# Scaling probabilities on GpSimd, copying turned probabilities on VectorE

## The reference

```python
pc = softmax(where(valid_c, q_raw @ kc.T * SCALE, NEG))        # compressed keys
ps = softmax(where(mask_s, q_rot @ k_slc.T * SCALE, NEG))      # selected blocks
pw = softmax(where(mask_w, q_rot @ k_win.T * SCALE, NEG))      # window of 512
o  = g[0] * (pc @ vc) + g[1] * (ps @ v_slc) + g[2] * (pw @ v_win)
```

## Time and profile before

| | |
|---|---|
| median of three executions | 3274.55 us |
| the profiled execution | 3271.69 us |
| its span in the trace | 3269.9 us |
| mean granted TensorE clock | 0.994 |
| PE busy | 3204.8 us (98%) |
| DVE busy | 1168.0 us (36%) |
| ACT busy | 1176.9 us (36%) |
| POOL busy | 1456.7 us (45%) |

### The profile page before, as it was taken

How to read it: one execution, slowest core, us unless ns; L and a number is a source line. 1 busy time by engine, 2 the same in 40 slices (tenths; PEclk the granted TensorE clock), 3 DMA queues, 4 the chain that set the end, 5 groups by cost and what they waited for, 6 DMA issues and landing times.

```text
span 3269.9 us, 39586 instructions
## 1 busy us (share of the span) xinstructions
PE 3204.8 (98%) x15940; PEld 2636.8 (81%) x15940; DVE 1168.0 (36%) x1727; ACT 1176.9 (36%) x1388; POOL 1456.7 (45%) x1112
## 2 busy tenths in 40 slices
PE   8999999999999999999999999999999989999998
PEld 7878888888888888888776888888888877788887
DVE  6534331343434112211847522114221375652212
ACT  4544332433443233222427332224222243743322
POOL 4335545433545444444550354454444373054443
PEclk9999999999999999999999999999999999999999
DMA  4213222211222222223320122222222242022222
GB/s 149 76 52 116 90 103 103 103 57 66 102 90 103 103 102 92 102 91 112 133 79 25 57 111 91 102 103 90 100 93 103 83 148 79 13 91 90 103 99 94
DMA packets 46234, 302.56 MB, mean 93 GB/s; under 512 B 5392, under 2 KB 7440, under 8 KB 10784
## 3 DMA queue, kind: packets, MB, share of 16 engines
q1 hardware_dynamic: 41040, 292.79, 25.0%
q10 hardware_dynamic: 5072, 7.96, 0.9%
HBM read 296.54 MB, written 2.10 MB: 91 GB/s over the span
## 4 chain that ended last, share of the span: by engine, by line
PE 90%; DVE 6%; ACT 2%; DMA 1%; issue 0%; SPq 0%; DVEq 0%; ACTq 0%
PE main L424 73%; PE main L441 3%; PE main L567 2%; PE main L1907 1%; PE main L526 1%; PE main L527 1%; PE main L531 1%; PE misc L527 1%; PE misc L526 1%; PE misc L531 1%; PE misc L484 1%; ACT b_p L2061 1%; PE misc L499 1%; DMA stage<-in_w 1%; DVE b_p L2283 1%; DVE b_flat L2146 1%
## 5 line engine op out<-in xcount | busy, mean ns | idle before, releaser
L2379 POOL TENSOR_TENSOR w_lo<-stage,w_hi 128x512 fp32r<-128x512 f32 x1104 | 1450.7, 1347 | 1778.8 <-ACT w_hi L637 1778.8
L424 PE MATMUL main<-h_hi,w_lo 128*128 128x512 f32 x2456 | 965.2, 393 | 7.3 <-DVE val L2093 5.5
L424 PE MATMUL main<-h_hi,w_hi 128*128 128x512 f32 x2456 | 959.3, 391 | 0.0
L424 PE MATMUL main<-h_lo,w_hi 128*128 128x512 f32 x2456 | 959.2, 391 | 0.0
L637 ACT ACTIVATE w_hi<-stage 128x2048 fp32r<-128x2048 f32 x276 | 525.0, 1910 | 408.3 <-DMA stage<-in_w 407.5
L424 PEld LDWEIGHTS main<-h_hi,w_lo 128*128 128x128 f32 x2456 | 463.6, 189 | 109.8 <-DVE val L2093 6.0
L424 PEld LDWEIGHTS main<-h_hi,w_hi 128*128 128x128 f32 x2456 | 463.0, 189 | 97.5
L424 PEld LDWEIGHTS main<-h_lo,w_hi 128*128 128x128 f32 x2456 | 463.6, 189 | 95.3 <-issue 0.5
L424 PE MATMUL main<-hid_hi,w_lo 128*128 128x512 f32 x1168 | 454.5, 389 | 0.0
L424 PE MATMUL main<-hid_hi,w_hi 128*128 128x512 f32 x1168 | 454.4, 389 | 0.0
L424 PE MATMUL main<-hid_lo,w_hi 128*128 128x512 f32 x1168 | 454.4, 389 | 0.0
(11 more groups left out here) (337 smaller groups left out, 3190.2 us busy)
## 6 DMA issues: line engine op xcount, KB each, us to landing
stage<-in_w SPq DMA_DIRECT2D x276, 1024.0 KB, 4.8
x<-in_xT SPq DMA_DIRECT2D x4, 512.0 KB, 7.6
out_x<-x ACTq DMA_DIRECT2D x4, 512.0 KB, 2.7
stage<-in_w SPq DMA_DIRECT2D x4, 256.0 KB, 7.8
b_r<-sq ACTq DMA_DIRECT2D x4, 256.0 KB, 6.8
b_r<-sq ACTq DMA_DIRECT2D x4, 255.5 KB, 8.2
ev_ws<-in_ev_ws ACTq DMA_DIRECT2D x1, 512.0 KB, 4.8
b_pos<-in_pos ACTq DMA_DIRECT2D x2, 256.0 KB, 2.8
```

The lines of the kernel that those rows point to most:

```text
L424: last = pe.matmul(acc[:, m, :], w[a], r[b], start=start and k == 0 and j == 0, stop=stop and k == nk - 1 and j == 2)
L2379: last = e.tensor_tensor(c.w_lo[:, s, k:k + 2, :].rearrange("p k n -> p (k n)"), c.stage[:, s, k * CW:(k + 2) * CW], c.w_hi[:, s, k:k + 2, ...
```

## The change

GpSimd does the scaling of line 2258. VectorE signals `a_share` behind the product with the gate, and GpSimd signals `a_norm` for each head as VectorE did. ScalarE copies only head 0 of each turned step (`a_copied`). VectorE copies head 1 in the new `turned`, behind `shares(s-1)` (`a_copied_b`). TensorE's waits follow the new counts. GpSimd's loop over chunks is cut in three: up to the attention of each layer it makes the low parts of all chunks whose high parts ScalarE has made by then, scales, and goes on.

```diff
@@ nsa_tensor, turn and values
-            pe.wait_ge(c.a_copied, 50 * l + 2 * s + hh + 1)
+            if hh == 0 or s == 0:
+                pe.wait_ge(c.a_copied, 26 * l + s + 1 + (s > 0 or hh))
+            else:
+                pe.wait_ge(c.a_copied_b, N_STEPS * l + s)
...
-        pe.wait_ge(c.a_copied, 50 * l + 2 * s + 4)
+        pe.wait_ge(c.a_copied, 26 * l + s + 3)
+        pe.wait_ge(c.a_copied_b, N_STEPS * l + s + 1)
@@ nsa_scalar
-            for hh in range(2):
-                act.wait_ge(c.a_probT, 50 * l + 2 * s - 2 + hh + 1)
-                act.activation(c.b_pT[:, (s - 2) % 2, hh, 0:w], c.m[hh][:, 0:w], ACT.Copy).then_inc(c.a_copied, 1)
+            act.wait_ge(c.a_probT, 50 * l + 2 * s - 1)
+            act.activation(c.b_pT[:, (s - 2) % 2, 0, 0:w], c.m[0][:, 0:w], ACT.Copy).then_inc(c.a_copied, 1)
@@ nsa_vector, shares
-        step(dve.tensor_tensor(den, den, gate, ALU.mult))
-        for hh in range(2):
-            for r, br in enumerate(brs):
-                p = step_prob(c, s, hh, r)
-                u = 2 * hh + br
-                last = dve.tensor_scalar(p, p, c.b_den[:, s % 4, u:u + 1], None, ALU.mult)
-            last.then_inc(c.a_norm, 1)
+        dve.tensor_tensor(den, den, gate, ALU.mult).then_inc(c.a_share, 1)
+
+    def turned(s):
+        i, m, brs = STEPS[s]
+        w = (i + 1) * P * len(brs)
+        dve.wait_ge(c.a_probT, 50 * l + 2 * s + 4)
+        dve.tensor_copy(c.b_pT[:, s % 2, 1, 0:w], c.m[1][:, 0:w]).then_inc(c.a_copied_b, 1)
...
+        if 2 <= s < N_STEPS + 2:
+            turned(s - 2)
@@ GpSimd
+def nsa_pool(pool, c, l):
+    for s in range(N_STEPS):
+        i, m, brs = STEPS[s]
+        pool.wait_ge(c.a_share, N_STEPS * l + s + 1)
+        for hh in range(2):
+            for r, br in enumerate(brs):
+                u = 2 * hh + br
+                p = step_prob(c, s, hh, r)
+                last = pool.tensor_scalar(p, p, c.b_den[:, s % 4, u:u + 1], None, ALU.mult)
+            last.then_inc(c.a_norm, 1)
...
+            made = seen = 0
+            for kind, kw in plan:
+                seen += PHASE_CHUNKS[kind]
+                if kind == "nsa":
+                    low_parts(made, seen - 4 + AHEAD)
+                    made = seen - 4 + AHEAD
+                    nsa_pool(pool, c, kw["l"])
+            low_parts(made, n_chunks)
```

More of the change, by code:

```diff
@@ L365, in __init__ @@
         self.a_norm = sem("a_norm")
+        self.a_share = sem("a_share")
+        self.a_copied_b = sem("a_copied_b")
         self.a_score = sem("a_score")
@@ L1828, in compressed_values @@
         if i == 3:
-            pe.wait_ge(c.a_copied, 50 * l + 2)
+            pe.wait_ge(c.a_copied, 26 * l + 2)
         if i == 2:
@@ L2324, in nsa_vector @@
     result_vector(dve, n, c, 1, norm, post)
+PHASE_CHUNKS = dict(first=0, even=14, ffn=34, odd=17, free=0, nsa=20, last=0)
+def nsa_pool(pool, c, l):
[8 more added lines that the diff above has]
+            last.then_inc(c.a_norm, 1)
 def build(nc, a, out, plan, n_chunks):
@@ L2383, in low_part, with low_parts @@
                 last.then_inc(c.w_lo_done, 1)
-            each_chunk(pool, n, low_part)
+            def low_parts(a, b):
+                while a < b and (a < RING or a % RING):
+                    low_part(pool, a, a % RING, a < RING)
+                    a += 1
+                rounds = (b - a) // RING
+                n.loop(pool, rounds, lambda e, i: [low_part(e, a + RING * i + s, s, False) for s in range(RING)])
+                for k in range(a + RING * rounds, b):
+                    low_part(pool, k, k % RING, False)
+            made = seen = 0
[6 more added lines that the diff above has]
+            low_parts(made, n_chunks)
         @block.tensor
```

## The result

The changed kernel takes 3307.41 us in the median of four runs (3303.69 to 3311.43), against 3274.92 for the kernel before, timed on the same chip (four runs, 3272.70 to 3278.95). The ratio is 1.0100, with a 95% interval of 1.0086 to 1.0114: slower by 1%, some 32.5 us. The prediction said 3273.2 and called slower the less likely side, and the time lies outside its range.

A forecast was written before the change was run, and what follows sets the result against it. TensorE, 98% busy, was taken as the bound. Per layer, +0.9 us before the last scores and -1.6 in the tail made -0.7, -1.4 in all: 3274.55 - 1.4, about 3273.2 us; 8-in-10 range 3265 to 3288, own range 3268 to 3279.

The forecast's parts named there:

- the price of GpSimd's scaling: In the attention: 0.68 us for 512 columns, 0.54, 0.39 and 0.25 for 384, 256 and 128; an estimate.
- The loop: Two attention steps through GpSimd: 2.22 + p us per first-tile step, p one scaling's time; binds from p = 0.89.
- slower rival: GpSimd's scaling as slow as its subtraction, 1.26 us, binds the attention steps: +7.2 us per layer, 3289 us; chance 0.27.
- step 1's turning: In step 2 on TensorE: second head ready at 1733.79, needed at 1733.37, so +0.4 us.
- the wait on the token sums: At step 4, VectorE's sums meet GpSimd's scalings: TensorE's token sums come 0.2 to 0.85 us later, taken as +0.5.
- Clock: TensorE's fall to 1.2 GHz in the second layer cost 1.7 us; may appear in both (+1.7) or move away (-1.7).
- The lock on hid_lo: Steps 12 to 15: VectorE's hid_lo, beside GpSimd's scalings, stretches from 0.75 to 0.9 us or more; 0.67 between two scalings.
- The tail: From the last scores to the end of the last values, 7.4 us: a lighter ScalarE gains 1.6 us per layer.
- The costs before the last scores: Delays in each attention stretch up to the scores of the last step: +0.9 us per layer.
- the weight loop's cut: GpSimd's weight subtractions, cut around the attention: the last ends 5 us ahead of the first scores, cost nothing.
- the copy of head 1: VectorE's copy from PSUM in attention steps: 0.61 us at 512 columns, with 0.7 us of slack.
- masks beside GpSimd: VectorE's attention masks, reading PSUM and one SBUF tile, were counted at 0.61 and 0.34 us, without stretching.

The follow-up runs named there:

- kernel with a quarter of the columns: The whole change, but each GpSimd scaling takes only the first quarter of its columns: 3275.21 us, ratio 1.0003 to the kernel before.
- late copies alone: Against the kernel before, VectorE still scales everywhere and copies head 1 only in steps 18 to 23: 3276.66 us, ratio 1.0004.

## Why the prediction was wrong, by its steps

**The step that failed is the price of GpSimd's scaling, and above all its bound.** "From above: GpSimd's subtraction ... 1.26" took for granted that an instruction with one streamed input can't be slower than one with two. It is: 1.55 against 1.23 for the product of two tiles, alone on the engine. The value 0.68 was then half of that bound. The price at 512, 384, 256 and 128 columns was 1.57, 1.32, 0.93 and 0.61 in place of 0.68, 0.54, 0.39 and 0.25. That this one number is the cause is shown from both sides: with a scaling of 0.66 the whole change costs nothing that can be measured, and with the dear scaling alone, the copy undone, the loss is whole. From the GPSIMD Engine Reference of the Trainium skill (section 3.1), the prediction worked out an estimate of some 0.6. The measured 1.55 contradicts it for this instruction, and the copy (0.57) is the only form that comes near.

**The loop held, where it was the bound.** It was priced as 2.22 + p per step in the first tile: with 1.56 that is 3.78, measured 3.37 and 4.26 in turn, 3.8 on the mean. Only those last two steps of the tile show it; the slower rival had counted six. Before them, step 1's turning waited for GpSimd (6.60 us from the scores at 1732.69 to the next, in place of 4.36: +2.2 where the prediction had +0.4), and the wait on the token sums gave the loop room. Those sums came 0.2 later behind their scores than before, where the prediction had 0.5. In the third tile 2.29 + 2 x 0.91 = 4.11, measured 3.85 and 4.26. The timeline of TensorE:

```profile
1787.12 1.13 PE L1778 MATMUL main<-b_k,b_qr 64*128 64x256 f32 x8
1788.46 0.55 PE L1792 MATMUL misc<-ident,b_p 128*128 128x128 f32 x3 [0.21 <-POOL b_p L2345]
1789.69 0.55 PE L1792 MATMUL misc<-ident,b_p 128*128 128x128 f32 x3 [0.68 <-POOL b_p L2345]
...
1790.97 1.13 PE L1778 MATMUL main<-b_k,b_qr 64*128 64x256 f32 x8
...
1795.23 1.14 PE L1778 MATMUL main<-b_k,b_qr 64*128 64x256 f32 x8
```

The slower rival was this very mechanism. Its 3289 was low above all because it went by 1.26: with the four measured prices its own sum gives some 14.5 per layer, about 3304 us. That is near the measured 3307.4, though not term by term: it has more in the first tile than the rows show, and less in the tail and for the clock (below). The prediction knew what would decide, and then let a false bound close the range.

**Where the 35.1 us of span went.** TensorE's waits on scalings rose from 4.9 to 25.4 us over both layers: +20.5. Both figures count idle time alone. TensorE ran at 1.2 GHz for 3.4 us in the stretches before and for 13.6 now, 10.2 more, which costs half of it, 5.1. Outside the stretches lie 3.2; the kernel with a quarter of the columns has more there (4.7) and no loss in its median. What is left, some 6 us, I put down to the restart of turning after each of 38 waits in place of 8. Eight blocks in one go take 1.09, split by a wait 2 x 0.66, so 0.23 more each, an estimated 7 us; that share was not isolated.

**Clock.** The prediction allowed +-1.7 us for one fall. There were three more, one of them in the middle of the loop, behind a wait of 1.22: scores that take 0.92 take 1.65.

```profile
1777.23 1.65 PE L1778 MATMUL main<-b_k,b_qr 64*128 64x384 f32 x4
```

The waits of TensorE were alike in the two layers, yet the first had one fall and the second three. So a new wait can cost more than itself, and this is a term the sum did not have.

**The lock on hid_lo** was expected to stretch it from 0.75 to 0.9 or more. It didn't: eight instructions, 741 to 832 ns, median 744. The second one of the first layer starts 0.82 behind the start of a running scaling and is not held up. What becomes longer is GpSimd's pair: 2.67 here and 3.01 in the step before, in place of 2.47. Timelines of VectorE and GpSimd:

```profile
1776.43 0.74 DVE L2315 SCALAR_TENSOR_TENSOR hid_lo<-b_y,par,hid_hi 128x512 fp32r<-128x512 f32 x1
```

```profile
1768.24 2.47 POOL L2345 TENSOR_SCALAR b_p<-b_p,b_den 128x384 f32<-128x384 f32 x2 [0.62 <-DVE b_den L2258]
1772.30 3.01 POOL L2345 TENSOR_SCALAR b_p<-b_p,b_den 128x384 f32<-128x384 f32 x2 [1.60 <-DVE b_den L2258]
1775.61 2.67 POOL L2345 TENSOR_SCALAR b_p<-b_p,b_den 128x384 f32<-128x384 f32 x2 [0.29 <-DVE b_den L2258]
```

The cost is real, 0 to 0.54 us per pair in the first layer where the prediction had 0.67, but falls on GpSimd. With the broadcast product in the scaling's place, both are stretched: hid_lo takes 0.88 to 1.07 in the first layer, and three of the four pairs 2.06 in place of 1.61. Again VectorE, then GpSimd:

```profile
1776.62 1.07 DVE L2360 SCALAR_TENSOR_TENSOR hid_lo<-b_y,par,hid_hi 128x512 fp32r<-128x512 f32 x1
```

```profile
1776.32 2.06 POOL L2395 TENSOR_TENSOR b_p<-b_p,b_den 128x384 f32<-128x384 f32 x2 [1.85 <-DVE b_den L2291]
```

So how long VectorE is held depends on which instruction GpSimd runs; why was not tested.

**The tail** was worth 1.6 us by the prediction. In the kernel with a quarter of the columns it is 7.2 (1796.67 to 1803.85) and with late copies alone 6.9, against 7.4: 0.2 to 0.5. In the first of them ScalarE was still in step 22 when the last scores started, at 1796.67. It worked without a gap until 1800.2, where the exponentials of step 23 end, 3.5 us behind the scores. The prediction had them done after 2.75, as it took ScalarE to be bound by the scores. That is 0.8 of the 1.6 us. The rest is in steps it priced too tight behind them, and was not taken apart. The costs before the last scores were too high in turn: from the first scores to the last are 74.9 us in that kernel against 74.8 before, +0.1 where the prediction had +0.9. The two errors of the sum largely cancel (-0.1 per layer in place of -0.7), so that this kernel lies within the range is in part luck. In the changed kernel the tail is 8.6, since four scalings of 0.6 in a row now stand in it (answers to the earlier trace rows):

```profile
1809.80 0.72 PE L1778 MATMUL main<-b_k,b_qr 64*128 64x128 f32 x8
...
1816.67 0.44 PE L1792 MATMUL misc<-ident,b_p 128*128 128x128 f32 x2 [0.73 <-POOL b_p L2345]
1817.04 1.34 PE L1804 MATMUL misc<-b_pT,b_va 128*64 128x128 f32 x16
```

**Right:** the weight loop's cut at nothing, the copy of head 1 without effect in the whole change (ratio 1.0100 with it, 1.0096 without), masks beside GpSimd not stretched (0.56 and 0.69), and that VectorE can take the copies once it is rid of the scalings.

## What to carry to other kernels

Before moving work to an engine, get the price of that very instruction: another operation of the same engine is no bound for it, not even one that reads more. When the price is unknown and the loop has a known threshold (here 0.89 us), the far side of the threshold belongs in the range with room above, as nothing measured closes it. And a job split between VectorE and GpSimd on tiles in SBUF may run one after the other, so splitting it helps less than the busy shares promise.

## What the runs showed of the hardware

- GpSimd on 128 x 512 float32 in SBUF, per instruction: scaling by a column 1.55 us, by a constant 1.47, product of two tiles 1.23, product with a broadcast column 1.01, copy 0.57. With 256 columns: 0.91, 0.83, 0.69, 0.58, 0.36. The dearest and the cheapest are both of one streamed input.
- VectorE's scaling of 512 columns (one streamed input in SBUF) takes 1.37 in place of 0.44 us where GpSimd's broadcast product runs beside it. Its masks, which read PSUM as well, do not change beside GpSimd's scaling (0.69 and 0.56), and hid_lo, with two SBUF inputs, takes 0.74 beside the scaling and up to 1.07 beside the product.
- TensorE's clock fell to 1.2 GHz behind some waits of 1.2 to 2.2 us, and not behind others of the same length. In the changed kernel each fall lasted 3.4 us and cost 1.7 on top of the wait; in the broadcast kernel, behind the 2.2 us, it lasted 6.8 and cost 3.4.
